# Five blocks of a macaron diffusion step become two: scans behind the input map, and one block from the heads' norm to the last norm

## The chip, the cores and the metric

The kernel runs on one core of a Trainium2 chip. The metric is device time in microseconds of that core for one execution. All data are float32; products that need more than the fast format gives are made of three matmuls of float32r halves (high and low parts).

## What is computed

One layer on 1152 tokens (128 context tokens, then 1024 latent tokens on a grid 64 wide), width 1024, 8 heads of 64, hidden width 2816:

```python
def trunk_layer(x, mod, s_fwd0, s_bwd0, grid, norm_w, ffn1_w13, ffn1_w2, ffn2_w13, ffn2_w2, mixer_params):
    m = mod[:, None].astype(x.dtype)
    h = rmsnorm(x, norm_w[0]) * (1.0 + m[:, :, 1]) + m[:, :, 0]
    x = x + 0.5 * m[:, :, 2] * swiglu(h, ffn1_w13, ffn1_w2)
    h = rmsnorm(x, norm_w[1]) * (1.0 + m[:, :, 4]) + m[:, :, 3]
    y, s_f, s_b = token_mixer(h, s_fwd0, s_bwd0, grid, *mixer_params)
    x = x + m[:, :, 5] * y
    h = rmsnorm(x, norm_w[2]) * (1.0 + m[:, :, 7]) + m[:, :, 6]
    x = x + 0.5 * m[:, :, 8] * swiglu(h, ffn2_w13, ffn2_w2)
    return x, s_f, s_b
...
    u = h @ w_in                       # in token_mixer
    o_f, s_f = wkv_scan(r_h, decay[:, :, 0], k_dir[:, :, 0], v_h, kk, a_h[:, :, 0], s_fwd0, False)
    o_b, s_b = wkv_scan(r_h, decay[:, :, 1], k_dir[:, :, 1], v_h, kk, a_h[:, :, 1], s_bwd0, True)
    o = o_f + o_b                      # then a norm per head, a bonus term and a gate g
    y_rwkv = o.astype(h.dtype) @ w_o_rwkv
    y_four = fourier_mix(f, grid) @ w_fourier
    merged = (gates[:, :, 0] * y_rwkv + gates[:, :, 1] * y_four).astype(h.dtype)
    return merged @ w_out, s_f, s_b
```

## The kernel before

Activations lie transposed: 128 channels on the partitions, the 1152 tokens along them, in three chunks of 384 tokens (`CH`) for the dense parts. `program` runs five stages. A stage is one block: each engine (PE, DVE, ACT, POOL and SP) has its own stream of instructions with hand-placed semaphore waits, and at the end of a block all engines meet at a barrier (`Kit.stage`); inside a block they meet only at semaphores.

1. `ffn` and `projection`, joined by `run`. The input map has 35 output rows, `p` = 0 to 34, each of three chunks with 24 matmuls (`product`, L1491). Rows 10 to 33 carry windows of six rows for each of four channel tiles `ct`, in which DVE makes the scans' four operands of a direction (`products`, L1358 to L1371) and SP stores them to the DRAM array `streams` (`store_operands`, L1109). The backward direction (d = 1) is made in window row 4, the forward one (d = 0) in window row 5, that is rows 32 and 33 for the last tile. PSUM banks 0 to 2 hold even rows, 3 to 5 odd ones.
2. `scans`: the RWKV recurrence by 128 tokens, 18 units (9 blocks of tokens in each direction, two chunks of 64 tokens in each), software-pipelined over slots `m` = -4 to 18. In slot m, unit m+4 gets its products within a chunk (`within`, PE L1915, and their masking `masked`, DVE L1803); POOL sends 16x16 blocks of them to DRAM and fetches them back as 64 lanes (`blocks_out` L1676, `lanes_in` L1684); unit m+3 has its triangular 16x16 blocks inverted by DVE (`row`, `corner`, L1826 to L1851); unit m+2 has them turned by ACT (`turn_block`) and taken through DRAM into `xy16` by SP (L1623, L1640), which also loads unit m+5 (`load_ar` L1604, `load_bkv` L1614); unit m+1 gets its inverse of 64x64 on PE, unit m its state update and output. POOL begins by clearing buffers (L1653 to L1659, semaphore `preset`), and PE, DVE and ACT wait for that; PE also waits for the initial states (`states_in`).
3. `head_norm`: norm per head, bonus and gate over 12 steps (`skewed`), beside it the feature half of the Fourier mixing (`channels`, 11 units on PE and ACT); SP loads its operands and the DFT matrices.
4. `fourier`: ACT and DVE split the matrices and `g` into halves (8 pairs, in `ORDER`), PE does a few two-column matmuls for the grid's edges (L2320, L2321), the context's 8 matmuls (L2325), then four groups q of 24 matmuls with 512 columns and two edge matmuls (L2337, L2342). ACT copies the odd part, DVE composes `whole`, ACT and DVE split it into `f_hi` and `f_lo` (L2403). SP reloads `x`.
5. `merge` (a `hidden_stage` on 8 tiles: products of both branches L936, times gates from DRAM, then `w_out` L951), the second `ffn` and `final_norm`, joined by `run`. It starts with SP's loads of raw weights (L755), their high halves (ACT L789) and low halves (DVE L825).

`run` writes the streams of several parts one after another on each engine, with no barrier between parts:

```python
def run(nc, parts):
    with nc.Block() as block:
        @block.sync
        def _(sp):
            for part in parts:
                part.sync(sp)
```

Of the kernel before, what the change touches and what calls it, by code (L numbers as in the profile page):

```python
# [691 lines left out]
def hidden_stage(kit, tag, tiles, ku, w_up, w_down, norm, moving, combine, gate, prev=None):  # L692
# [21 lines left out]
    with ExitStack() as ctx:  # L714
# [36 lines left out]
        def sync(sp):  # L751
# [29 lines left out]
        def scalar(act):  # L781
# [52 lines left out]
        def vector(dve):  # L834
# [36 lines left out]
            else:  # L871
                first_low(dve)

# [43 lines left out]
        def tensor(pe):  # L917
# [3 lines left out]
            def up(i, par, c, early):  # L921
# [9 lines left out]
                for j, q in enumerate("ab"):  # L931
                    hi, lo = moving[j]
                    for k in range(ku):
# [101 lines left out]
def projection(kit, mix, x_saved, cst, kd_sum, streams, v_back, g_last, prev):  # L1035
# [31 lines left out]
    with ExitStack() as ctx:  # L1067
# [22 lines left out]
        def sync(sp):  # L1090
# [24 lines left out]
            for p in range(J_END):  # L1115
# [8 lines left out]
                else:  # L1124
                    sp.wait_ge(evicted, p * 3 + 3)
# [40 lines left out]
                if w == 5:  # L1166
                    store_operands(ct, 0)
            for par in range(2):
                sp.wait_ge(row_stored[par], rows_before(par, J_END))
                sp.wait_ge(stored[par], 64 * CT)  # L1170
# [129 lines left out]
        def vector(dve):  # L1300
# [99 lines left out]
            for p in range(J_END):  # L1400
# [21 lines left out]
                if w == 5:  # L1422
# [99 lines left out]
    stage.engines(sync, scalar, vector, gpsimd, tensor)  # L1522
    prev.follow = norm
# [8 lines left out]
def scans(kit, cst, streams, v_rows, n_blocks, x_blocks, o, g_last, states_in, states_out):  # L1532
# [11 lines left out]
             "lane_step", "turned_block", "full6", "free6", "full7", "free7", "u_done", "u_act", "u_dve", "z_done",  # L1544
# [11 lines left out]
    with ExitStack() as ctx:  # L1556
        buf = lambda name, shape, dt=F32: ctx.enter_context(nc.sbuf_tensor("sc_" + name, shape, dt))
        masks = buf("masks", [P, MASK_W])
        ar = buf("ar", [P, AR, 2, CT, P])

        bk, vs = buf("bk", [P, BKV, CT, 4, CK]), buf("vs", [P, BKV, CT, P])
# [4 lines left out]
        q_plus, x_wide, y_wide, y = (buf(n, [P, HEADS, CK]) for n in ("q_plus", "x_wide", "y_wide", "y"))  # L1566
        a_tall = buf("a_tall", [P, CT, 2, HD])

        kb, uv = buf("kb", [P, 2, CT, 2, P]), buf("uv", [P, 2, CT, 2, 2, HD])
        wa = buf("wa", [P, 2, CT, CK])  # L1570
        lane_n, lane_x = buf("lane_n", [64, 2, BL * (BL + 1)]), buf("lane_x", [64, 2, 2, BL * (BL + 1)])
        prod, half_way = buf("prod", [64, 512]), buf("half_way", [64, 8, 8])
        z = buf("z", [P, 2, 2, CT, HD])
        zg = buf("zg", [P, 2, CT, HD])
        block = ctx.enter_context(nc.Block())
# [21 lines left out]
        @block.sync  # L1597
        def _(sp):
            sp.dma_start(masks[:], kit.dram["masks"]).then_inc(S["masks_in"], 16)

            def load_ar(k):
# [1051 lines left out]
```

## Time and profile before

| | |
|---|---|
| median of three runs | 3000.89 us (2998.18 to 3003.07) |
| profiled execution, its own time | 2998.46 us |
| its span, first to last instruction | 2996.6 us |
| PE busy | 2815.8 us (94%) |
| DVE, ACT, POOL busy | 1540.7, 805.5, 472.6 us |
| mean granted TensorE clock | 0.974 |
| block 1 to 2 (input map to scans) | last eviction starts 1445.04, first instruction of the next block 1450.35 |
| block 3 to 4 (heads' norm to Fourier) | last POOL operation starts 1852.11, next block 1854.20 |
| block 4 to 5 (Fourier to merge) | last DVE operation starts 1896.31, next block 1898.50 |

A busy engine is one with an instruction in flight, so gaps are what to look for. In a timeline row the columns are start (us), duration (us), engine, line, operation, output<-inputs, shapes and count; in brackets the idle time before it and what ended that. In the rows of DMA issues on SP and POOL the duration is that of issuing, and the landing comes later. The clock is given as a share of 2.4 GHz: 0.50 is 1.2 GHz.

### The profile page before, as it was taken

What the parts mean: (1) busy time and instruction counts of PE and PEld (TensorE: products, weight loads), DVE (VectorE), ACT (ScalarE), POOL (GpSimd) and SP (SyncE); (2) the same over time, 40 slices, a digit from 0 to 9 for tenths busy, and PEclk for the clock granted to TensorE, in tenths of its full rate; (3) what the DMA queues carried; (4) which work ended last, traced back from release to release, by engine and by line L of the source; (5) the groups of instructions that cost most, each with busy time, mean ns of one, the idle gap of its engine ahead of it and who ended that gap; (6) DMA issues with size and microseconds to landing.
All of it is one profiled execution on the core that took longest, in us unless ns stands there. A gap on an engine that the chain in (4) does not pass through costs nothing. (4 is left out here: it accounts for less than half of the span.)

```text
span 2996.6 us, 53527 instructions
## 1 busy us (share of the span) xinstructions
PE 2815.8 (94%) x21936; PEld 2684.9 (90%) x21936; DVE 1540.7 (51%) x2777; ACT 805.5 (27%) x1409; POOL 472.6 (16%) x569
## 2 busy tenths in 40 slices
PE   6999999999998998999599976899899999999998
PEld 3999999999997988999587865799799999999997
DVE  4456665566536345642377757445633333333335
ACT  4211111111115233444165544212511111111111
POOL 4101101110005010122234314122500000000001
PEclk9999999999999999999699998999999999999999
DMA  6122222222203434444545432321111111111112
GB/s 268 57 71 84 72 82 84 84 83 72 69 8 116 129 107 147 138 143 143 174 110 115 100 121 95 114 70 57 36 43 43 42 42 42 42 42 42 42 42 70
DMA packets 186302, 257.67 MB, mean 86 GB/s; under 512 B 98048, under 2 KB 136064, under 8 KB 184480
## 3 DMA queue, kind: packets, MB, share of 16 engines
q1 hardware_dynamic: 173280, 227.86, 23.3%
q0 software_dynamic: 12864, 27.54, 2.8%
q8 instruction: 119, 1.95, 0.3%
q14 instruction: 39, 0.32, 0.0%
HBM read 200.23 MB, written 55.12 MB: 85 GB/s over the span
## 5 line engine op out<-in xcount | busy, mean ns | idle before, releaser
L840 DVE SCALAR_TENSOR_TENSOR x<-bank,gate,x 128x128 f32<-128x128 f32 (+1 forms) x832 | 409.6, 515 | 200.0 <-PE bank L951 199.4
L1002 ACT ACTIVATE act_out_ffn<-bank 128x384 f32<-128x384 f32 x132 | 64.9, 491 | 1267.9 <-PE bank L936 1267.9
L1005 DVE TENSOR_TENSOR g_ffn<-act_out_ffn,bank 128x384 f32<-128x384 f32 x132 | 73.1, 554 | 616.6 <-ACT act_out_ffn L1002 616.6
L936 PE MATMUL bank<-h_hi_ffn,wlo_a_ffn 128*128 128x384 f32 x1056 | 359.2, 340 | 13.7 <-DVE h_lo_ffn L663 7.3
L936 PE MATMUL bank<-h_lo_ffn,whi_a_ffn 128*128 128x384 f32 x1056 | 356.8, 338 | 0.0
L936 PE MATMUL bank<-h_hi_ffn,whi_a_ffn 128*128 128x384 f32 x1056 | 356.7, 338 | 0.0
L936 PE MATMUL bank<-h_hi_ffn,whi_b_ffn 128*128 128x384 f32 x1056 | 355.2, 336 | 0.0
L936 PE MATMUL bank<-h_hi_ffn,wlo_b_ffn 128*128 128x384 f32 x1056 | 355.2, 336 | 0.0
L936 PE MATMUL bank<-h_lo_ffn,whi_b_ffn 128*128 128x384 f32 x1056 | 355.2, 336 | 0.0
L951 PE MATMUL bank<-g_hi_ffn,wlo_d_ffn 128*128 128x384 f32 x1056 | 354.4, 336 | 0.0
L951 PE MATMUL bank<-g_lo_ffn,whi_d_ffn 128*128 128x384 f32 x1056 | 353.1, 334 | 0.0
L951 PE MATMUL bank<-g_hi_ffn,whi_d_ffn 128*128 128x384 f32 x1056 | 353.1, 334 | 0.0
L1491 PE MATMUL bank<-h_hi_mix,wlo_in 128*128 128x384 f32 x840 | 292.9, 349 | 10.9 <-DVE wlo_in L1292 6.1
L1491 PE MATMUL bank<-h_lo_mix,whi_in 128*128 128x384 f32 x840 | 285.9, 340 | 0.0
L1491 PE MATMUL bank<-h_hi_mix,whi_in 128*128 128x384 f32 x840 | 285.5, 340 | 0.0
L936 PEld LDWEIGHTS bank<-h_hi_ffn,wlo_a_ffn 128*128 128x128 f32 x1056 | 199.9, 189 | 15.6 <-DVE h_lo_ffn L663 9.7
L936 PEld LDWEIGHTS bank<-h_lo_ffn,whi_a_ffn 128*128 128x128 f32 x1056 | 199.9, 189 | 0.1
L936 PEld LDWEIGHTS bank<-h_hi_ffn,whi_a_ffn 128*128 128x128 f32 x1056 | 199.7, 189 | 0.0
L951 PEld LDWEIGHTS bank<-g_lo_ffn,whi_d_ffn 128*128 128x128 f32 x1056 | 198.3, 188 | 0.5
L951 PEld LDWEIGHTS bank<-g_hi_ffn,wlo_d_ffn 128*128 128x128 f32 x1056 | 198.3, 188 | 0.5
L936 PEld LDWEIGHTS bank<-h_hi_ffn,whi_b_ffn 128*128 128x128 f32 x1056 | 198.6, 188 | 0.0
L936 PEld LDWEIGHTS bank<-h_lo_ffn,whi_b_ffn 128*128 128x128 f32 x1056 | 198.5, 188 | 0.0
(300 smaller groups left out, 4936.5 us busy)
## 6 DMA issues: line engine op xcount, KB each, us to landing
ada_beside_ffn<-in_ada_w POOLq DMA_DIRECT2D x96, 256.0 KB, 3.5
raw_a_ffn<-in_ffn_w SPq DMA_DIRECT2D x44, 512.0 KB, 4.5
raw_b_ffn<-in_ffn_w SPq DMA_DIRECT2D x44, 512.0 KB, 5.0
raw_d_ffn<-in_ffn_w SPq DMA_DIRECT2D x44, 512.0 KB, 3.6
raw_in<-in_w_in SPq DMA_DIRECT2D x35, 512.0 KB, 5.1
mix<-row_out SPq DMA_DIRECT2D x23, 576.0 KB, 3.2
sc_ar<-streams SPq DMA_DIRECT2D x36, 256.0 KB, 3.5
gates<-mix SPq DMA_DIRECT2D x16, 576.0 KB, 5.0
```

The lines of the kernel that those rows point to most:

```text
L840: ins = nc.vector.scalar_tensor_tensor(xs, kit.banks[4 + d % 4][:, a:b], kit.gate[:, gate, d, cond:cond + 1], xs, ALU.mult, ALU.add)
L936: mm = nc.tensor.matmul(kit.banks[2 * slot + j][:, 0:CH], w[q][:, par, cols], v[:, k, toks], start=(k == 0 and m == 0), stop=(k == ku - 1 ...
L951: mm = nc.tensor.matmul(kit.banks[4 + d % 4][:, 0:CH], w["d"][:, par, cols], v[par][:, c], start=(par == 0 and m == 0), stop=(par == 1 and ...
L1002: return self.nc.scalar.activation(out, a, ACT.Silu)
L1005: self.nc.vector.tensor_tensor(g32, act_out, b, ALU.mult).then_inc(g32_ready, 1)
L1491: mm = nc.tensor.matmul(bank[3 * par + c][:, 0:CH], wt[:, par, cols], v[:, k, toks], start=(k == 0 and m == 0), stop=(k == KT - 1 and m == 2))
```

## The change

The scans become a `Part` that follows the input map in the same block, and head norm, Fourier, merge, second FFN and last norm share one block. The barriers between go; waits on the semaphores of the part in front take their place.

- `projection`: the last tile's forward operands are made one row earlier (row 32 instead of 33). Before it waits for the last row, SP waits until all operands are stored and then loads unit 0, the masks and the initial states of the scans. The scans' buffers are laid out anew so that these lie clear of what the input map still uses. The last waits for stores move behind the scans (`rows_out`).
- `scans`: PE starts when the row before the last has been evicted; its waits for `preset` and `states_in` move to the first matmuls that need them. POOL's clearing starts when the last product is done. For units 0 and 1, ACT issues half of `blocks_out`. In slots -2 and -1, SP loads unit m+5 behind the `xy16` transfers, not ahead of them.
- `fourier`: PE does the context first, then the edges in the order q = 0, 3, 1, 2 with waits for the head norm's last users of those banks. ACT's splits wait for `gated` and `with_bonus`. SP's reload of `x` waits for `lo_ready`.
- `merge`: the first weights are loaded when the fourth Fourier group is done on PE.

```diff
@@ projection, sync
+                    if p == J_END - 1:
+
+                        for d in range(2):
+                            sp.wait_ge(stored[d], 64 * CT)
+                        stage.follow_loads(sp)
                     sp.wait_ge(evicted, p * 3 + 3)
...
-                if w == 5:
+                if w == (4 if ct == CT - 1 else 5):
                     store_operands(ct, 0)
@@ projection, vector
-                if w == 5:
+                if w == (4 if ct == CT - 1 else 5):
                     products(ct, 0)
@@ scans, sync
+        def first_loads(sp):
+            load_unit(sp, 0)
             sp.dma_start(masks[:], kit.dram["masks"]).then_inc(S["masks_in"], 16)
...
+        prev.follow_loads = first_loads
...
-                k = m + 5
...
+                if m >= 0 or m < -2:
+                    load_unit(sp, m + 5)
...
+                if -2 <= m < 0:
+
+                    load_unit(sp, m + 5)
@@ scans, gpsimd
+            for d in range(2):
+                pool.wait_ge(prev.stored[d], 64 * CT)
+            pool.wait_ge(prev.proj_done, J_END * NC)
...
-                for c in range(2):
+                for c in range(1 if k < 2 else 2):
@@ scans, scalar
+                if m + 4 < 2:
+                    act.wait_ge(S["am_ready"], 4 * (m + 4) + 4)
+                    for b in range(4):
+                        act.dma_start(*blocks_of(m + 4, 1, b)).then_inc(S["n_out_act"], 16)
@@ scans, tensor
-            pe.wait_ge(S["preset"], 7)
-            pe.wait_ge(S["states_in"], 32)
+
+            pe.wait_ge(prev.evicted, J_END * NC - 3)
@@ fourier, tensor
+            pe.wait_ge(prev.s["dft_in"], 32)
+            pe.wait_ge(prev.s["g_ready"], 11)
...
+            for q in (0, 3, 1, 2):
...
+                if q < 3:
+                    pe.wait_ge(prev.s[("rooted", "bonus_v", "gated")[q]], prev.steps)
@@ fourier, scalar
+            act.wait_ge(prev.s["with_bonus"], prev.steps)
+            act.wait_ge(prev.s["gated"], prev.steps)
@@ hidden_stage, sync, scalar and tensor
+            if after:
+
+                sp.wait_ge(after.s["done"], FG)
...
+                act.wait_ge(after.s["out_lo"], FG)
+                act.wait_ge(after.s["ctx_lo"], 1)
...
+                    if after and early and (par, c) == (0, 0):
+
+                        pe.wait_ge(after.before["lo_ready"], CT * NC)
+                        pe.wait_ge(*((after.s["out_lo"], FG) if j else (after.s["whole"], 5)))
@@ program
-                run(nc, [first, projection(kit, mix, x_saved, cst, kd_sum, streams, v_back, g_last, first)])
-            with kit.stage():
-                scans(kit, cst, streams, (mix[2 * CT:3 * CT], v_back), n_blocks, x_blocks, o, g_last,
-                      dram["states"], states_out)
+                second = projection(kit, mix, x_saved, cst, kd_sum, streams, v_back, g_last, first)
+                third = scans(kit, cst, streams, (mix[2 * CT:3 * CT], v_back), n_blocks, x_blocks, o, g_last,
+                              dram["states"], states_out, second)
+                run(nc, [first, second, third])
...
+            run(nc, [of_heads, mixed, merged, last, final_norm(kit, y_out, last)])
```

SP in slots -2 and -1 of the scans, before (`x_blocks` is unit 0's turned block on its way out, `sc_xy` its way back, `sc_ar`, `sc_bk`, `sc_vs` the load of unit 3, then the same of units 1 and 4):

```order
L1623 DMA x_blocks<-sc_lane_x 64x2x256
L1604 DMA sc_ar<-streams 128x4x128 x2
L1614 DMA sc_bk<-streams 128x4x64 x2
L1614 DMA sc_bk<-streams 128x4x128
L1614 DMA sc_vs<-v_back 128x4x64 x2
L1640 DMA sc_xy<-x_blocks 16x16x16 x8
```

and in the changed kernel:

```order
L1663 DMA x_blocks<-sc_lane_x 64x2x256
L1674 DMA sc_xy<-x_blocks 16x16x16 x8
L1630 DMA sc_ar<-streams 128x4x128 x2
L1640 DMA sc_bk<-streams 128x4x64 x2
L1640 DMA sc_bk<-streams 128x4x128
L1640 DMA sc_vs<-v_back 128x4x64 x2
```

The load of unit 3 has moved behind the eight transfers back of unit 0.

SP where the input map ends, in the changed kernel (the first row is the store of row 33, the last store of `mix` that of row 34; between them stands the load of unit 0, the masks and the states, which before stood behind the barrier):

```order
L1145 DMA mix<-row_out 128x1152
L1630 DMA sc_ar<-streams 128x4x128 x2
L1640 DMA sc_bk<-streams 128x4x64 x2
L1640 DMA sc_bk<-streams 128x4x128
L1640 DMA sc_vs<-mix 128x4x64 x2
L1653 DMA sc_masks<-in_masks 128x192
L1655 DMA sc_z<-in_states 128x256 x2
L1145 DMA mix<-row_out 128x1152
```

The load of the first unit has moved ahead of the last row's store.

PE at the end of the heads' norm, before (`hn_g_up` is the gate's matmul of the last step; the branches are the end of one block and the start of the next):

```order
L2155 MATMUL bank<-hn_gd,hn_g_up 128x384
L2096 UNCONDITIONAL_BRANCH
L2313 UNCONDITIONAL_BRANCH
L2320 MATMUL bank<-fo_dft,fo_g 128x2 x4
L2321 MATMUL bank<-fo_dft,fo_g_left 128x2
...
L2325 MATMUL bank<-fo_dft_ctx,fo_g_ctx 128x128 x8
```

and in the changed kernel:

```order
L2203 MATMUL bank<-hn_gd,hn_g_up 128x384
L2364 MATMUL bank<-fo_dft_ctx,fo_g_ctx 128x128 x8
L2374 MATMUL bank<-fo_dft,fo_g 128x2 x4
L2375 MATMUL bank<-fo_dft,fo_g_left 128x2
```

The eight context matmuls now come first, directly behind the last gate.

## Rows read from the trace of the kernel before

**Rows 1.** The page's 40 slices of 75 us: granted TensorE clock in tenths

```profile
PEclk9999999999999999999699998999999999999999
```

**Rows 2.** Stretches around joints: us, busy by engine (count), clock, DMA share, GB/s

```profile
1846.00:1850.00 4.00, 0.91 (x2) 0.30 (x2) 3.97 (x5) 1.23 (x2) 1.97 (x3) 0.62 0.00 0
1892.00:1903.00 11.00, 0.90 (x4) 0.29 (x2) 3.96 (x10) 2.91 (x4) 0.00 (x0) 0.63 0.26 85
1907.00:1909.00 2.00, 2.00 (x9) 2.00 (x9) 0.00 (x0) 0.00 (x0) 0.00 (x0) 0.65 1.04 426
```

**Rows 3.** Timeline of SP where the input map ends

```profile
1436.22 1.20 SPq L1109 DMA_DIRECT2D streams<-wo_keep  x1
```

**Rows 4.** Timeline of POOL where the scans begin

```profile
1450.35 0.56 POOL L1653 MEMSET sc_z<- 128x256 f32 x2 [50.23 <-POOLq L86]
...
1455.40 0.16 POOL L1659 MEMSET sc_lane_x<- 64x16 f32 x2
...
1465.91 4.24 POOL L1676 DMA_DIRECT2D n_blocks<-sc_nkr  x8 [6.62 <-DVE sc_nkr L1803]
```

**Rows 5.** Timeline of PE in the scans' first slots

```profile
1458.62 2.08 PE L1915 MATMUL bank<-sc_ar,sc_bk 64*128 64x128 f32 x16 [13.62 <-DMA sc_z<-in_states]
...
1489.88 2.08 PE L1915 MATMUL bank<-sc_ar,sc_bk 64*128 64x128 f32 x16 [4.67 <-DMA sc_vs<-v_back]
1492.63 0.37 PE L1928 MATMUL bank<-sc_xy,sc_n 64*64 64x64 f32 x2 [0.67 <-DMA sc_xy<-x_blocks]
```

**Rows 6.** Timeline of DVE from the input map's end on

```profile
1425.86 1.23 DVE L1292 TENSOR_TENSOR wlo_in<-raw_in,whi_in 128x1024 fp32r<-128x1024 f32 x1 [5.69 <-ACT whi_in L1177]
...
1460.85 1.29 DVE L1803 TENSOR_TENSOR sc_nkr<-bank,sc_masks 128x512 f32<-128x512 f32 x2 [28.50 <-PE bank L1915]
...
1473.72 0.16 DVE L1826 COPY sc_lane_x<-sc_lane_n 64x2 f32<-64x2 f32 x1 [1.69 <-DMA sc_lane_n<-n_blocks]
```

**Rows 7.** Timeline of SP in slot -2 of the scans

```profile
1481.61 0.62 SPq L1623 DMA_DIRECT2D x_blocks<-sc_lane_x  x1
...
1485.18 1.13 SPq L1614 DMA_DIRECT2D sc_vs<-v_back  x2
1486.35 4.57 SPq L1640 DMA_DIRECT2D sc_xy<-x_blocks  x8
```

**Rows 8.** DMA issues 1440 to 1512 us: queue, count, KB each, median us to landing

```profile
sc_vs<-v_back SPq DMA_DIRECT2D x4, 128.0 KB, 3.9
...
x_blocks<-sc_lane_x SPq DMA_DIRECT2D x3, 128.0 KB, 2.4
```

**Rows 9.** ACT's copy once per slot: min/median/max ns, first and last start

```profile
L1699 ACT ACTIVATE sc_a_tall<-bank x18: 597/597/605, 1499.6 to 1760.3; 128x512 f32<-128x512 f32 x18
```

**Rows 10.** Timeline of PE, heads' norm to merge

```profile
1846.07 0.91 PE L2155 MATMUL bank<-hn_gd,hn_g_up 128*128 128x384 f32 x2 [2.30 <-DVE x L2242]
1854.25 1.84 PE L2320 MATMUL bank<-fo_dft,fo_g 128*128 128x2 f32 x8 [7.26 <-PEq L86]
...
1863.47 3.79 PE L2325 MATMUL bank<-fo_dft_ctx,fo_g_ctx 128*128 128x128 f32 x16
1866.91 0.72 PE L2337 MATMUL bank<-fo_dft_hi,fo_g_lo 128*128 128x512 f32 x1
...
1892.51 0.39 PE L2342 MATMUL bank<-fo_left_rows,fo_left_hi 2*128 2x512 f32 x1
1903.36 0.66 PE L936 MATMUL bank<-rwkv_hi,wlo_a_merge 128*128 128x384 f32 x1 [10.46 <-DVE wlo_b_merge L825]
```

**Rows 11.** Timeline of ACT where the Fourier stage begins

```profile
1854.22 0.63 ACT L2348 ACTIVATE fo_dft_hi<-fo_dft 128x512 fp32r<-128x512 f32 x1 [2.20 <-PEq L86]
```

**Rows 12.** Timeline of DVE, last bonus, last Fourier half, first weights of the merge

```profile
1850.91 0.56 DVE L2242 TENSOR_TENSOR x<-bank,hn_v 128x384 f32<-128x384 f32 x1 [0.92 <-POOL hn_v L2259]
...
1896.31 1.23 DVE L2403 TENSOR_TENSOR fourier_lo<-fo_whole,fourier_hi 128x1024 fp32r<-128x1024 f32 x1 [1.12 <-ACT fourier_hi L2348]
...
1902.52 0.69 DVE L825 TENSOR_TENSOR wlo_b_merge<-raw_b_merge,whi_b_merge 128x512 fp32r<-128x512 f32 x1
```

More of the change, by code:

```diff
@@ L689, in vector, with hidden_stage @@
                 normed(m + DEEP)
-def hidden_stage(kit, tag, tiles, ku, w_up, w_down, norm, moving, combine, gate, prev=None):
+def hidden_stage(kit, tag, tiles, ku, w_up, w_down, norm, moving, combine, gate, prev=None, after=None):
     nc = kit.nc
@@ new lines, in blocks_of, with load_ar, load_bkv @@
+        def blocks_of(k, c, b):
+            at = 64 * c + BL * b
+            return (n_blocks[k, :, c, b].rearrange("h s t -> s h t"),
+                    nkr[at:at + BL, k % NKR, :, :, c, 0, BL * b:BL * b + BL].rearrange("s e x t -> s (e x) t"))
+        def load_ar(sp, k):
+            for q in range(2):
+                sp.dma_start(*ar_of(k, q)).then_inc(ar_loaded[k % AR], 16)
+        def load_bkv(sp, k):
+            at = slice(k // 2 * P, k // 2 * P + P)
+            b, key, v = (src[:, :, at].rearrange("c p t -> p c t")
+                         for src in (streams[k % 2, 2], streams[k % 2, 3], v_rows[k % 2]))
+            pieces = [(bk[:, k % BKV, :, 3 * c], b[:, :, CK * c:CK * (c + 1)]) for c in range(2)]
+            both = bk[:, k % BKV].rearrange("p c q t -> p c (q t)")[:, :, CK:3 * CK]
+            for dst, src in pieces + [(both, key)] + [(vs[:, k % BKV, :, half(1 - c)], v[:, :, half(c)]) for c in range(2)]:
+                sp.dma_start(dst, src).then_inc(bkv_loaded[k % BKV], 16)
@@ L2084, in _ @@
                     ins.then_inc(S["wy_done"], 1)
+    part = Part()
+    part.engines(sync, scalar, vector, gpsimd, tensor)
+    return part
 def head_norm(kit, cst, mix, o, kd_sum, o_hi, o_lo, waves):
@@ L2243, in _, with gpsimd @@
             skewed([(0, center), (2, bonus), (3, gated), (1, normed)])
-            dve.wait_ge(s["lo_ready"], steps)
-        @block.gpsimd
-        def _(pool):
+        def gpsimd(pool):
             for ct in range(CT):
@@ L2265, in _ @@
             skewed([(0, weighted), (2, with_bonus), (3, low)])
+    part_of = Part()
+    part_of.engines(sync, scalar, vector, gpsimd, tensor)
+    part_of.s, part_of.steps = s, steps
+    return part_of
 class Waves:
@@ L2322, in _ @@
                                  skip_group_check=True)
-            for q in range(FG):
-                for p in range(2):
-                    ins = nc.tensor.matmul(bank[3][:, q * P:(q + 1) * P], waves.g_ctx[:, p, q], waves.dft_ctx[:, p],
-                                           start=(p == 0), stop=(p == 1))
-            ins.then_inc(s["ctx_done"], 1)
             for q in range(FG):
@@ L2404, in _, with gpsimd @@
                     .then_inc(s["out_lo"], 1)
-            dve.wait_ge(s["out_lo"], FG)
-            dve.wait_ge(s["ctx_lo"], 1)
+        def gpsimd(pool):
+            pass
+    part = Part()
+    part.engines(sync, scalar, vector, gpsimd, tensor)
+    part.s, part.before = s, prev.s
+    return part
 class Merge:
```

152 lines of the change are left out of this document (70 added, 82 removed).

## Prediction

> **What bounds the kernel now.** The page's clock row comes first: 40 slices, 9 in all but three, and one 6, at 1423 to 1498 us, where the input map gives way to the scans [rows 1]. With PE 94% busy, the dense stages offer nothing to this change. It can win only where PE stands still, at the joints, so I read the timelines of all engines there, each from the last work of one stage to the first full work of the next.
>
> At the first joint POOL begins to clear buffers at 1450.35, though the input map's last eviction began at 1445.04, and is done at 1455.56 [rows 4]. PE does its first product of a unit at 1458.62, held by the initial states, which SP asks for behind the barrier [rows 5]. DVE masks it at 1460.85 [rows 6], POOL spends 4.24 us on eight issues of blocks [rows 4], and the inversion starts at 1473.72 [rows 6]. From there one engine hands to the next until the slots run. ACT's copy, once per slot, goes from 1499.6 to 1760.3 in 17 steps, 15.3 us each [rows 9]: the recurrence is a chain, and the change keeps its order from slot 0 on.
>
> At the heads' norm's end PE's last gate starts at 1846.07; then it idles 7.26 us, does edges for 9.22 us (1854.25 to 1863.47), the context in 3.44 (to 1866.91), and meets its first dense matmul at 1866.91 [rows 10]. ACT waits for the same barrier [rows 11]. From Fourier to merge, DVE's last half starts at 1896.31 and runs 1.23; PE gets its first weights at 1903.36 after 10.46 us idle, DVE's low half being last [rows 10, 12]. The barrier between heads' norm and scans stays.
>
> **The change, joint by joint.** Sums are against the profiled execution, 2998.46 us.
>
> *Input map to scans.* POOL's clearing takes 5.21 us (1450.35 to 1455.56) [rows 4]. Started at 1445.1, when the last product is done, it ends at 1450.3. SP's stores of operands end about 1438 (the last issue begins at 1436.22 and takes 1.20) [rows 3]. The loads of unit 0, now issued behind them, take 4.1 us to issue (1486.35 - 1481.61 - 0.62 for unit 3) and 3.9 to land [rows 7, 8]; with masks and states they are in by about 1447, and PE's first products (2.08 us) are done under the clearing. So the first mask can start at 1450.3 in place of 1460.85: 10.5 us gained. POOL and ACT now share unit 0's eight issues: half of 4.24 is 2.1; I give back 0.3, since ACT's half needs the last mask as POOL's does. The inversion then starts 12.3 us sooner, near 1461.4.
>
> Against that: in slot -2 SP issued unit 0's block at 1481.61, unit 3's loads, the last two (1.13 together) at 1485.18, and the transfers back (4.57) at 1486.35 [rows 7]; PE took unit 3 at 1489.88, held 4.67 by those loads [rows 5], 8.3 us after the first issue. Now the loads stand behind the transfers back, which wait for the block to land: 2.4 [rows 8], eight issues 4.57, the loads up to the last one 1485.18 - 1481.61 - 0.62 = 2.95, and 0.57, its landing 3.9 [rows 8]: 14.4 us. Unit 3 comes 6.1 us later against unit 0. It holds what stands behind it on PE, unit 0's inverse among them; the 0.67 that PE waited for the transfer back [rows 5] goes. Joint: -12.3 + 6.1 - 0.7 = **-6.9 us**. Unit 4 is needed a slot of 15.3 later, and covered. Bounds: nothing given back and the transfer gained is -13; the loads as late again is -1.
>
> The transfers out and back have no load beside them now. The rows' 2.4 us is taken with such loads. The Trainium skill (DMA: Bandwidth & Descriptors, Latency and other measured facts) puts the access to HBM at 0.2 us on average and 2 us at high load. By the page, an estimate, the block would land up to 1.8 sooner, and the joint give -8.7. No row of before shows that transfer alone.
>
> Making the last tile's forward operands in row 32 costs nothing: DVE idles 5.69 us before 1425.86 [rows 6], and the products are off PE's path. Were that cover gone, four products of 1152 columns, 1.4 each by the 1.23 that 1024 take [rows 6], would delay PE 5.5 at most. The row stores at the scans' end lie behind the barrier's own work, on SP alone. ACT's four new issues per unit, 2.1 us, fall in slots in which it idles.
>
> *Heads' norm to Fourier.* PE can go on after 1846.98 with the context, 3.44 us, to 1850.4, then 9.22 of edges to 1859.6; the last of its new semaphores comes when DVE's gating ends, 1850.91 + 0.56 [rows 12], ahead of need. ACT's splits wait for the same and begin about 1852.0 in place of 1854.22 [rows 11], and stay ahead of PE. That is 7.3 sooner than 1866.91. But the clock is 0.62 on average in 1846 to 1850 [rows 2], and PE's ten microseconds of two-column matmuls follow it. Before, the 128-column context stood directly ahead of the dense part; now the edges do. So the first dense matmuls run at 1.2 GHz for longer. The merge shows the price: its dense work begins at 1903.36 [rows 10], and the clock still averages 0.65 over 1907 to 1909, PE being full [rows 2], so about 5 us are done at half speed, against some 0.5 here before. 4.5 us at half speed lose 2.2. **-5.1 us**; bounds -8.4 (clock up, ACT's start sets it) and -4.5.
>
> *Fourier to merge.* The last low half ends at 1897.54 [rows 12]. The raw weights, asked for when PE's fourth group is done, 1892.51 + 0.39 [rows 10], land by 1896.8 at the latest, by the 2.4 to 3.9 of rows taken elsewhere [rows 8]; ACT's high halves are done about as DVE's last Fourier half is, and DVE's two low halves behind its last Fourier half, 0.69 each or less [rows 12], let PE start at 1899.0 (1897.54 + 0.69 + 0.69, and 0.1). That is **-4.4 us**. PE is busy 0.90 of 11 us at a clock of 0.63 before [rows 2], and would still start low. Bounds -4 and -6.5 (clock up: half of 5 us less).
>
> Sum: -6.9 - 5.1 - 4.4 = **-16.4 us**, 2982.1 in the profiled execution's terms. That execution is 2.4 under the median of 3000.89; the four executions shown average 3000.2. Minus 16.4 that is 2983.7, and I say **2983.5 us**.
>
> **The rivals.**
>
> *More of the scans' start is gained.* If the loads queued behind the transfers are not what PE next needs, because DVE's inversion of unit 1 or the slot itself is last, the joint gives -13: total -22.5, 2977.5 us. For it: 4.67 us of PE's wait [rows 5] fell in a stretch where PE has little. Against: `within` of unit 3 stands ahead of unit 0's inverse on PE.
>
> *The clock comes back.* With idle gaps of 6 in place of 10.46 us [rows 10], it may hold: -6.9 - 8.4 - 6.5 = -21.8, 2978 us. Against: 0.62 right after the gate [rows 2].
>
> *The scans keep less.* If two loads hold PE, unit 4's too, joint one gives -3: -12.5, 2987.5 us.
>
> *The change does not do what it says.* The early loads wait for stores; every microsecond by which they land after 1450.3 is one lost. Were they as late as the states were (PE at 1458.62, 8 us), the joint gives about +1: total -8.5, 2991.5 us. Against: the stores' last issue at 1436.22 leaves 14 us.
>
> *Slower: SP becomes the bound of the slots.* The scans now hold the row stores' semaphores, a new layout of buffers and a loop changed on SP. Were each of the 17 steps [rows 9] longer, 0.96 us would cancel the whole, and from 1.3 us (16.4 + 6 = 22.4) it is slower by over 0.2%; at 1.6 us a step it gives +10.8, 3011 us. Against: SP's slot of 1481.61 to 1490.92 is 9.3 us of work [rows 7] in 15.3, and the order from slot 0 on is unchanged.
>
> **How the numbers follow.** A measurement of this kernel tells about 0.2%, 6 us, from no change. Forecast 0.60, with 2979 to 2988 as its own range; more gained 0.14; clock back 0.10; less kept 0.07; not as said 0.03; slots longer 0.06, half of it under 1.3 us a step, counted as no change. All but the last are faster by over 6 us: faster 0.94, same 0.03, slower 0.03. The range 2973 to 2989.5 reaches to both gains together and to the smaller one.
>
> **What would show it.** DVE's first mask near 1450.3 behind POOL's clearing; the first inversion near 1461.4; PE's unit 3 waiting for its loads, 14 us behind the first block's issue; ACT's copies still 15.3 apart, 6.9 us earlier. PE's first dense Fourier matmul 13 us after the last gate, in place of 20.8, at a clock of 0.5, and the merge's first matmul 1.5 us after DVE's last Fourier half. The forecast is wrong if the copies' distance changes, if unit 3 waits for nothing, or if the clock is near 1 at either of the later joints.

## The result and the profile after

| | before | changed |
|---|---|---|
| median | 3000.89 us | 2982.28 us (five runs, 2978.81 to 2985.01) |
| ratio, 95% interval | | 0.9934 (0.9916 to 0.9951) |
| span of the profiled execution | 2996.6 us | 2978.6 us |
| PE busy, its share | 2815.8 us (94%) | 2812.2 us (94%) |

The change gave 18.6 us of the medians and 18.0 us of the spans. PE's busy time fell by 3.6, so most of the gain came out of PE's idle time, at the joints. The table adds the two spans up, from mark to mark. Every mark is the start or end of a row. The *inversion* is DVE's work on the triangular blocks (its copy into `sc_lane_x`), the *last gate* is the head norm's last pair of `hn_g_up` matmuls, and a *Fourier group* is one of the four rounds of dense 512-column matmuls.

| stretch | before | changed | difference |
|---|---|---|---|
| start to the input map's last matmul | 1445.00 | 1443.28 | -1.7 |
| from there to DVE's first mask | 15.85 | 5.46 | -10.4 |
| to the first inversion | 12.87 | 12.37 | -0.5 |
| to PE's first `sc_xy` matmul (unit 0's inverse) | 18.91 | 23.92 | +5.0 |
| to ACT's first copy per slot | 6.92 | 5.20 | -1.7 |
| to ACT's second copy | 14.55 | 17.41 | +2.9 |
| to its last | 246.22 | 247.13 | +0.9 |
| to the last gate of the heads' norm | 85.75 | 85.96 | +0.2 |
| to the end of the first Fourier group | 27.58 | 19.42 | -8.2 |
| to the end of the fourth | 19.25 | 19.21 | 0.0 |
| to the merge's first matmul | 10.46 | 5.95 | -4.5 |
| to the end | 1093.24 | 1093.29 | 0.0 |

The first row is not the change's: the difference is the same 1.75 us in ACT's rows from 1145 us on, long before anything that the diff touches. Over the kernels below, whose input map is the same, the mark lies anywhere from 1443.2 to 1445.7.

POOL at the scans' start (start, duration, instruction, and in brackets the idle time before it with its releaser):

```profile
1443.43 0.56 POOL L1693 MEMSET sc_z<- 128x256 f32 x2 [45.03 <-PE bank L1509]
...
1448.48 0.16 POOL L1699 MEMSET sc_lane_x<- 64x16 f32 x2
...
1453.79 2.17 POOL L1714 DMA_DIRECT2D n_blocks<-sc_nkr  x4 [4.58 <-DVE sc_nkr L1843]
1459.03 0.55 POOL L1722 DMA_DIRECT2D sc_lane_n<-n_blocks  x1 [3.07 <-DMA n_blocks<-sc_nkr]
```

The clearing starts 0.15 us behind the last matmul, where it stood 5.35 behind [rows 4], and DVE's first mask follows it at once:

```profile
1424.14 1.23 DVE L1310 TENSOR_TENSOR wlo_in<-raw_in,whi_in 128x1024 fp32r<-128x1024 f32 x1 [0.41 <-ACT whi_in L1195]
1448.74 1.29 DVE L1843 TENSOR_TENSOR sc_nkr<-bank,sc_masks 128x512 f32<-128x512 f32 x2 [23.37 <-POOL sc_lane_x L1699]
...
1461.11 0.16 DVE L1866 COPY sc_lane_x<-sc_lane_n 64x2 f32<-64x2 f32 x1 [1.19 <-DMA sc_lane_n<-n_blocks]
```

Ahead of 1424.14 DVE idled 0.41 us, where it idled 5.69 [rows 6]: the operands now made in row 32 fill that gap, as predicted, and the input map's end is not later for it.

PE's first product is done far ahead of that, since SP has fetched its operands while the input map still ran. SP, from the last store of the scans' operands on:

```profile
1429.00 1.18 SPq L1121 DMA_DIRECT2D streams<-wo_keep  x1
...
1434.94 0.99 SPq L1630 DMA_DIRECT2D sc_ar<-streams  x2
...
1440.00 0.91 SPq L1655 DMA_DIRECT2D sc_z<-in_states  x2
...
1468.94 0.62 SPq L1663 DMA_DIRECT2D x_blocks<-sc_lane_x  x1
1471.36 3.79 SPq L1674 DMA_DIRECT2D sc_xy<-x_blocks  x8
1475.19 1.01 SPq L1630 DMA_DIRECT2D sc_ar<-streams  x2
...
1477.96 1.45 SPq L1640 DMA_DIRECT2D sc_vs<-v_back  x2
```

The last store is issued at 1429.00, 7.2 us sooner than before [rows 3]. The load of unit 0 is issued from 1434.94 to 1439.3, the states to 1440.9. Later, unit 0's turned block goes out at 1468.94, comes back from 1471.36 on, and only then are the loads of unit 3 issued. PE shows what that costs:

```profile
1443.21 1.16 PE L1954 MATMUL bank<-sc_ar,sc_bk 64*128 64x128 f32 x16
...
1483.02 2.08 PE L1954 MATMUL bank<-sc_ar,sc_bk 64*128 64x128 f32 x16 [10.40 <-DMA sc_vs<-v_back]
```

It waited 10.40 us for unit 3, 14.1 behind the block's issue (1468.94 to 1483.02), in place of 4.67 and 8.3 [rows 5, 7]. ACT's copy, once per slot (min, median and max in ns, first and last start):

```profile
L1736 ACT ACTIVATE sc_a_tall<-bank x18: 597/597/598, 1490.2 to 1754.8; 128x512 f32<-128x512 f32 x18
```

By the table the 17 steps sum to 264.5 us, against 260.8, and 2.9 of the 3.8 lie in the first of them.

PE from the last gate to the end of the first Fourier group:

```profile
1840.73 0.91 PE L2203 MATMUL bank<-hn_gd,hn_g_up 128*128 128x384 f32 x2 [2.31 <-DVE x L2287]
1841.48 3.29 PE L2364 MATMUL bank<-fo_dft_ctx,fo_g_ctx 128*128 128x128 f32 x16
1844.56 1.28 PE L2374 MATMUL bank<-fo_dft,fo_g 128*128 128x2 f32 x8
...
1846.08 1.05 PE L2374 MATMUL bank<-fo_dft,fo_g 128*128 128x2 f32 x8
...
1847.37 1.05 PE L2374 MATMUL bank<-fo_dft,fo_g 128*128 128x2 f32 x8
...
1848.66 1.87 PE L2374 MATMUL bank<-fo_dft,fo_g 128*128 128x2 f32 x8
...
1850.97 0.80 PE L2386 MATMUL bank<-fo_dft_hi,fo_g_lo 128*128 128x512 f32 x1
...
1858.53 0.50 PE L2386 MATMUL bank<-fo_dft_hi,fo_g_lo 128*128 128x512 f32 x1 [0.24 <-DVE fo_g_lo L2429]
...
1859.76 0.39 PE L2391 MATMUL bank<-fo_left_rows,fo_left_hi 2*128 2x512 f32 x1
```

The context's matmuls come right behind the gate. Three of the four edge groups take 1.28 to 1.05 us, the fourth 1.87, as all four did before [rows 10]. The clock shows why (columns as in [rows 2]):

```profile
1841.00:1845.00 4.00, 4.00 (x21) 3.73 (x21) 3.62 (x4) 1.25 (x3) 1.97 (x3) 0.60 0.01 4
1845.00:1849.00 4.00, 4.00 (x30) 3.90 (x30) 1.79 (x4) 3.04 (x7) 2.50 (x3) 0.93 0.16 13
1851.00:1855.00 4.00, 4.00 (x11) 3.17 (x11) 3.70 (x7) 4.00 (x9) 0.00 (x0) 0.50 1.02 415
1885.00:1889.00 4.00, 3.69 (x12) 3.72 (x13) 0.21 (x1) 0.00 (x0) 0.00 (x0) 0.50 1.02 411
```

The 0.60 during the context is a mean: the clock was still at 1.00 for the last gate, fell to 0.50 within the context, and was back at 1.00 in the first edge group. It is 0.93 in the first three, and 0.50 again when the dense matmuls begin. Between the fourth group and the merge:

```profile
1878.97 0.39 PE L2391 MATMUL bank<-fo_left_rows,fo_left_hi 2*128 2x512 f32 x1
1885.31 0.66 PE L948 MATMUL bank<-rwkv_hi,wlo_a_merge 128*128 128x384 f32 x1 [5.95 <-DVE wlo_a_merge L830]
```

PE idles 5.95 us in place of 10.46 [rows 10]; the merge still begins at 0.50.

### The profile page after: what moved, and what is told of

It is laid out like the page before. It is cut to its first block and busy times, and to the rows that moved or that the text cites. A ratio compares the mean times of both kernels' runs of the same rounds, so it can differ in the third digit from the quotient of the medians.

```text
span 2978.6 us, 53460 instructions
## 1 busy us (share of the span) xinstructions
PE 2812.2 (94%) x21936; PEld 2680.6 (90%) x21936; DVE 1541.9 (52%) x2777; ACT 805.3 (27%) x1409; POOL 468.7 (16%) x561
## 3 DMA queue, kind: packets, MB, share of 16 engines
q8 instruction: 119, 1.95, 0.3%
## 5 line engine op out<-in xcount | busy, mean ns | idle before, releaser
L948 PE MATMUL bank<-h_hi_ffn,wlo_a_ffn 128*128 128x384 f32 x1056 | 358.8, 340 | 11.3 <-DVE h_lo_ffn L663 4.5
L948 PEld LDWEIGHTS bank<-h_hi_ffn,wlo_a_ffn 128*128 128x128 f32 x1056 | 199.6, 189 | 13.2 <-DVE h_lo_ffn L663 6.8
```

The source lines that it names most:

```text
L948: mm = nc.tensor.matmul(kit.banks[2 * slot + j][:, 0:CH], w[q][:, par, cols], v[:, k, toks], start=(k == 0 and m == 0), stop=(k == ku - 1 ...
```

## The experiments

Executions of one kernel lie 1 to 10 us apart, so medians of four or five runs do not tell 3 us apart. The kernel before was run again beside each set (medians 3000.63, 2998.53 and 2999.36 us), so where two changed kernels are compared, their ratios are the fairer numbers. Most verdicts below are read from stretches between marks in the profiles, one profile for each kernel. Three are used: *front*, from the input map's last matmul to ACT's second copy per slot (69.10 before, 64.36 changed); *gate to group*, from the last gate to the end of the first Fourier group (27.58 and 19.42); *gap*, from the fourth group's end to the merge's first matmul (10.46 and 5.95).

**1. Units 3 and 4 loaded ahead of the transfers back.**

```diff
-                if m >= 0 or m < -2:
-                    load_unit(sp, m + 5)
+                load_unit(sp, m + 5)
...
-                if -2 <= m < 0:
-                    load_unit(sp, m + 5)
```

> The changed kernel with one part undone: in slots -2 and -1 SP again issues the loads of units 3 and 4 ahead of the transfers back. Theory A (PE's wait for unit 3's load is what the new order costs, 14.1 us behind the first block's issue against 8.3 before): unit 3's first product comes again about 8.3 us behind that issue, 5.8 sooner than in the changed kernel, but the transfer back then lands about 4 us later than it does there, so unit 0's inverse starts near 1480 in place of 1485.0 and the second of ACT's copies per slot is 3 to 5 us sooner. Time 2978 to 2980 us. Theory B (DVE's inversions and POOL's blocks set the first slots whatever SP does): that copy moves by less than 1 us, time 2982 us, or later by the transfers' delay.

Median 2974.40 us, ratio to the kernel before 0.9915 (0.9892 to 0.9937). PE's unit 3:

```profile
1477.46 2.08 PE L1950 MATMUL bank<-sc_ar,sc_bk 64*128 64x128 f32 x16 [4.74 <-DMA sc_vs<-v_back]
```

That is 8.4 us behind the block's issue at 1469.05. Unit 0's inverse starts 11.3 us behind it in place of 16.1, front 57.25. Against 64.36 that is 7.1 less; against the mean of the four kernels with the front unchanged (64.36 and the 62.13, 60.33 and 60.99 of experiments 5 to 7: 61.95) 4.7. Experiment 12 has the same edit, and there the front was 59.06, 2.9 below that mean. Theory A holds, and this part of the change costs more than it brings: 3 to 5 us.

**2. The same loads still earlier**, behind that of unit 2 (`if m == -3: load_unit(sp, 3); load_unit(sp, 4)`).

> The changed kernel with the loads of units 3 and 4 issued in slot -3, right behind that of unit 2 and ahead of the first block's turn, into buffers that are free then. Theory A: PE waits for neither load; unit 0's inverse waits only for its transfer back, 8 to 9 us behind the first block's issue, near 1477.5 in place of 1485.0; the second of ACT's copies comes 5 to 8 us sooner, time 2975 to 2977 us. Theory B: less than 1 us of it arrives. If the early loads delay the small block transfers, the first inversion itself (12.5 us behind the first mask) comes later.

Median 2977.21 us, ratio 0.9925 (0.9905 to 0.9945). PE waited for neither load, and the inverse started 8.2 us behind the block's issue, as theory A has it. But the first inversion came 15.5 us behind the first mask, not 12.4: POOL's store of the blocks met the loads.

```profile
1455.92 2.16 POOL L1714 DMA_DIRECT2D n_blocks<-sc_nkr  x4 [4.57 <-DVE sc_nkr L1843]
1462.39 0.54 POOL L1722 DMA_DIRECT2D sc_lane_n<-n_blocks  x1 [4.31 <-DMA n_blocks<-sc_nkr]
```

POOL waits 4.31 us for them to land, where 3.07 stood. Front 60.06, 4.3 us less than changed and not the 5 to 8 expected: part of the gain went back into the small transfers.

**3. POOL alone issues the block stores** (ACT's four issues and their semaphore taken out, POOL's loop over both chunks).

> The changed kernel with POOL issuing all eight block stores of units 0 and 1, ACT none. As predicted the shared issue is worth 1.8 us from first mask to first inversion. The trace of the changed kernel shows that stretch as 12.37 us (1448.74 to 1461.11) against 12.87 before (1460.85 to 1473.72), 0.5 us. So by the prediction the stretch goes to 14.2 us, by the trace to 12.9. Time within 2 us of the changed kernel either way.

Median 2979.42 us, ratio 0.9934 (0.9916 to 0.9953). The stretch from first mask to first inversion is 12.98 us. Sharing the issues is worth 0.6 us, not the 1.8 predicted: POOL issues for 4.23 us and then waits 1.50 for the landing here, 2.17 and 3.07 in the changed kernel. The issues took half the time, and most of the rest went into the wait.

Experiment 11 shows what the wait was for. It shares the issues too, but holds unit 2's load until these blocks have landed:

```profile
1455.74 2.17 POOL L1714 DMA_DIRECT2D n_blocks<-sc_nkr  x4 [3.52 <-DVE sc_nkr L1845]
...
1459.40 0.55 POOL L1722 DMA_DIRECT2D sc_lane_n<-n_blocks  x1 [1.50 <-DMA n_blocks<-sc_nkr]
```

POOL waits 1.50 us, and the stretch is 11.09 us, 1.9 less than with POOL alone. In the changed kernel SP issues unit 2's load from 1449.67 to 1455.0, just ahead of and beside the shared stores (1453.79 to 1455.96); POOL's last stores in experiment 3 go out some 2 us later. So the predicted 1.8 us is there when no load is in flight, and unit 2's load takes most of it away.

**4. The masks do not wait for the clearing.**

```diff
@@ scans, vector
-            dve.wait_ge(S["preset"], 7)
+            for d in range(2):
+                dve.wait_ge(prev.stored[d], 64 * CT)
+            dve.wait_ge(prev.proj_done, J_END * NC)
...
                 if s == 6:
+                    if k == 0:
+                        dve.wait_ge(S["preset"], 7)
```

> The changed kernel with DVE's masks no longer waiting for POOL's clearing, only for the input map's last product and stores; the first inversion waits for the clearing instead. If the clearing is what the scans' start waits for, the first mask comes about 5 us sooner (right behind PE's first product, near 1444 in place of 1448.7), the first inversion 4 to 5 us sooner, and the time is 4 to 5 us less, 2978 us. Rival: PE's first products or the loads of units 1 and 2 are late next, or PE's hold for unit 3 (its loads stand behind the block's transfer) passes it on in full; if unit 1's load is late the gain is 1 to 2 us.

Median 2978.18 us, ratio 0.9929 (0.9909 to 0.9949). The first mask starts 1.23 us behind the last matmul, the first inversion 16.47 behind it (DVE, then PE):

```profile
1445.55 1.29 DVE L1845 TENSOR_TENSOR sc_nkr<-bank,sc_masks 128x512 f32<-128x512 f32 x2 [19.16 <-PE bank L1958]
...
1460.79 0.15 DVE L1870 COPY sc_lane_x<-sc_lane_n 64x2 f32<-64x2 f32 x1
```

```profile
1444.24 1.16 PE L1958 MATMUL bank<-sc_ar,sc_bk 64*128 64x128 f32 x16
...
1454.60 2.08 PE L1958 MATMUL bank<-sc_ar,sc_bk 64*128 64x128 f32 x16 [6.54 <-DMA sc_vs<-v_back]
```

Of 4.2 us gained at the mask, 1.4 arrive at the inversion: PE waits 6.54 us for unit 1's load, and unit 0's blocks land among the loads (POOL waits 4.31 us, as in experiment 2). The rival named beforehand, a gain of 1 to 2 us, is what happened.

**5. Edges ahead of the context**, as before the change.

> The changed kernel with the edges' two-column matmuls again ahead of the context's in the Fourier stage, nothing else changed. Theory A (the splits set the end of the first Fourier group: its last operand half was ready only when PE reached it, 0.24 us waited for DVE at 1858.53, so a slow clock on PE costs nothing there): the stretch from the last gate to the end of the first group stays 19.0 us within 1 us. Theory B (PE with its clock sets it): edges at 1.2 GHz cost 3 us more than the mix seen, dense matmuls at 2.4 GHz give 2.4 back or less, and the order moves the end by more than 1 us.

Median 2978.05 us, ratio 0.9926 (0.9909 to 0.9944). Gate to group 20.28 us: 0.9 more. All four edge groups ran at 1.2 GHz, and the dense matmuls sooner at 2.4. That is within the 1 us of theory A, but DVE was not waited for at all in the first group, so PE set the end here. The clock, 2 us behind the last gate and 14 us behind it (columns as in [rows 2]):

```profile
1844.66:1846.66 2.00, 2.00 (x10) 1.97 (x10) 1.89 (x4) 0.75 (x2) 0.18 (x1) 0.50 0.00 0
1856.66:1858.66 2.00, 2.00 (x9) 1.55 (x9) 2.00 (x5) 1.81 (x4) 0.00 (x0) 0.87 1.03 424
```

The other kernels with the changed order show both. PE in experiment 1:

```profile
1834.58 3.13 PE L2360 MATMUL bank<-fo_dft_ctx,fo_g_ctx 128*128 128x128 f32 x16
1837.50 1.71 PE L2370 MATMUL bank<-fo_dft,fo_g 128*128 128x2 f32 x8
...
1839.65 1.87 PE L2370 MATMUL bank<-fo_dft,fo_g 128*128 128x2 f32 x8
```

Here the clock fell and did not come up again in the context (1.71 and 1.87 for the first two edge groups), nothing waited for a split, and gate to group was 21.78; so it was in experiment 12. In experiment 2 the clock did not fall in the context at all:

```profile
1837.04:1839.04 2.00, 2.00 (x14) 1.73 (x15) 2.00 (x1) 0.50 (x1) 1.79 (x2) 1.00 0.00 0
```

PE waited for DVE's halves there, and gate to group was 19.42. The nine other kernels that keep order and joint, the changed one and experiment 2 among them, lie at 19.40 to 20.34: seven at 19.40 to 19.42, all with a wait for DVE's halves in the first group, and two (experiments 4 and 9) at 20.3 with none. So the splits set a floor of 19.4, and the clock adds 0 to 2.4 us. The order by itself is not shown to cost anything, since its 20.28 lies inside that spread. Why the clock was back by the first edge group in nine executions and not in two was not settled.

**6. Extra matmuls in the gap**: 26 of 512 columns into bank 4, read from the heads' halves; they compute nothing that is used.

```diff
@@ fourier, tensor, at its end
+            pe.wait_ge(prev.s["lo_ready"], prev.steps)
+            pe.wait_ge(s["whole"], 5)
+            for _ in range(26):
+                nc.tensor.matmul(bank[4][:], kit.spare[:, 0, 0:P], kit.spare[:, 0, 0:512], start=True, stop=True)
```

> The changed kernel with 26 extra 512-column matmuls at the end of PE's Fourier part, about 5.6 us of work without use, into a bank that nobody reads, in the 5.95 us in which PE idles ahead of the merge. If the idle PE is what makes the clock fall, it stays at 2.4 GHz and the merge's first 4 us of work at 1.2 GHz take 2: 2 to 2.4 us less up to the second row of the merge, time 2980 us. If the clock falls all the same, or the extra work ends later than the weights come, 0 or up to 1 us more.

Median 2975.64 us, ratio 0.9926 (0.9909 to 0.9942). The gap and the merge's start, 7 and 4 us:

```profile
1876.00:1883.00 7.00, 7.00 (x31) 5.26 (x30) 4.06 (x10) 2.70 (x4) 0.00 (x0) 1.00 0.72 249
1883.00:1887.00 4.00, 4.00 (x25) 4.00 (x25) 0.00 (x0) 0.00 (x0) 0.00 (x0) 1.00 1.03 420
```

The clock is 1.00 where it was 0.50, and from the merge's first matmul to its second row of output it took 13.17 us in place of 15.17, the 2.0 us expected, with the gap unchanged at 5.96. The kernels without extra work, before and after the change, lie at 14.6 to 15.9 in that stretch (mean 15.4), those with it (experiments 10 to 12 too) at 13.2 to 14.4 (mean 13.7). In experiment 10 PE then waited 1.63 us for the second row's weights, so a part of the gain met a wait.

**7. The two rear barriers back.**

```diff
@@ program
-            run(nc, [of_heads, mixed, merged, last, final_norm(kit, y_out, last)])
+            tail = final_norm(kit, y_out, last)
+            run(nc, [of_heads])
+            run(nc, [mixed])
+            run(nc, [merged, last, tail])
```

> The changed kernel with the two barriers back between heads' norm, Fourier and merge, the order on each engine unchanged. The two stretches from last gate to the end of the first Fourier group (19.0 us, 27.2 before) and from last Fourier group to first merge matmul (6.3, 10.9 before) should give back most of 8.2 and 4.5 us if the barrier is the cause: 10 to 13 us more, time 2992 to 2995 us. If the order on PE (context ahead of edges, which brings the clock up) gave a part of the 8.2, that part stays: then 7 to 9 us more.

Median 2988.76 us, ratio 0.9968 (0.9957 to 0.9979). Gate to group 25.63, gap 9.79: 6.2 and 3.8 us given back, 10.0 in all. The ratios give 10 us too (0.9968 against 0.9934), the low end of the 10 to 13 expected; the median rose by 6.5, less than expected. The remaining 1.95 us of the first and 0.7 of the second are not the barriers': the order on PE and the waits, and what a stage's end did beyond the barrier, were not tried for them.

What a barrier costs here is mostly what it holds back. At the first, POOL's last operation ran to 1841.94, and only then could PE begin the context and ACT the splits (1842.70):

```profile
1840.95 0.99 POOL L2306 TENSOR_TENSOR rwkv_lo<-x,rwkv_hi 128x384 fp32r<-128x384 f32 x1 [0.27 <-ACT rwkv_hi L2249]
1842.74 3.36 PE L2364 MATMUL bank<-fo_dft_ctx,fo_g_ctx 128*128 128x128 f32 x16 [6.52 <-PEq L108]
```

At the second, SP could ask for the merge's weights only at 1884.70, when DVE's last half was done (1884.43); without the barrier it asked at 1879.39, as soon as the fourth group had ended.

**8. A barrier back between input map and scans**, early loads kept (the last hunk of experiment 9's diff).

> The changed kernel with a barrier back between input map and scans; unit 0's loads, masks and states stay early. By the prediction the loads' share is what held PE before, and the barrier's own share is small: clearing starts when the last eviction is over, about 5 us later than now (before: 1450.35 against an eviction from 1445.04, in place of 0.1 us after the last product), so the scans' start gives back 5 to 6 us and no more, time 2987 to 2988 us. Rival: without the barrier's gain nothing of the 12.6 us is left, time 2994 us.

**9. The same, and unit 0's loads, masks and states behind the barrier.**

```diff
@@ projection, sync
-                        stage.follow_loads(sp)
@@ scans, sync
         def sync(sp):
+            first_loads(sp)
@@ program
-                run(nc, [first, second, third])
+                run(nc, [first, second])
+                run(nc, [third])
```

> The changed kernel with a barrier between input map and scans and, behind it, unit 0's loads, masks and states (the run before this one with a barrier alone had them early: 6.8 us from the input map's last matmul to the first mask, in place of 5.5). By the kernel before (first product 8.3 us behind the barrier, mask 10.5) the loads are the larger share: from last matmul to first mask 11.5 to 12 us, so early loads are worth 5 us and the barrier 1.3. The rest of the 15.9 us of the kernel before (4 us) would be what its block end waits for: the stores' landing and the clearing of semaphores. Rival: the 15.9 comes back in full, then the barrier's cost depends on what hangs on it.

Medians 2979.40 us, ratio 0.9938 (0.9921 to 0.9955), and 2988.30 us, 0.9961 (0.9948 to 0.9973). DVE's first mask with the barrier alone, then PE's first product and DVE's first mask with the loads late too:

```profile
1450.27 1.29 DVE L1843 TENSOR_TENSOR sc_nkr<-bank,sc_masks 128x512 f32<-128x512 f32 x2 [24.70 <-POOL sc_lane_x L1699]
```

```profile
1454.75 2.08 PE L1954 MATMUL bank<-sc_ar,sc_bk 64*128 64x128 f32 x16 [9.64 <-DMA sc_vs<-mix]
```

```profile
1456.97 1.29 DVE L1843 TENSOR_TENSOR sc_nkr<-bank,sc_masks 128x512 f32<-128x512 f32 x2 [29.78 <-PE bank L1954]
```

From last matmul to first mask: 5.46 us changed, 6.77 with the barrier, 11.86 with late loads, 15.85 in the kernel before. So of the 10.4 us gained, the barrier between blocks is 1.3, the early loads 5.1, and the last 4.0 is what the old stage's end did besides. The trace places it ahead of the scans' first instruction, which starts 1.54 us behind the last matmul (1445.11) in experiment 9 and 5.35 behind it in the kernel before [rows 4]:

```profile
1446.65 0.56 POOL L1693 MEMSET sc_z<- 128x256 f32 x2 [46.42 <-POOLq L108]
```

What it consists of is read from the program: waiting for the last stores, clearing the stage's semaphores, and a second barrier behind that (`all_engine_barrier` in `Kit.stage`). These were not tried apart. My expectation for the barrier, 5 to 6 us, was wrong: I had taken the old stage's end for the price of a barrier.

**10 to 12. Towards a faster version.** The tenth holds unit 2's load on SP until the first lanes have landed (`sp.wait_ge(n_in[0], 16)` in slot -3), together with experiments 1, 4 and 6; the eleventh adds unit 1's load to the early ones; the twelfth is experiments 1 and 6 alone.

> Four edits on the changed kernel: masks wait no longer for the clearing; SP holds unit 2's load until the first lanes have landed (so that the small block transfers meet fewer loads: they took 4.3 us to land with three loads issued on end, 1.5 before); units 3 and 4 are loaded ahead of the transfers back; 26 extra matmuls ahead of the merge. From last matmul to first inversion 17.8 us now, 16.5 with early masks alone: expected 13 to 14.5. From last matmul to ACT's second copy 60 to 64 now; expected 53 to 55. With 2 us at the merge, 10 us less in all: 2971 us. If unit 1's load, behind the last row's store, still holds PE (6.5 us with early masks), the first inversion comes no sooner than 16 us.

> As the four edits, and unit 1's load too ahead of the last row's store. PE's hold for unit 1 (6.5 us with early masks) should go, and the landing of unit 0's blocks meet no large load: first inversion 12 to 13 us behind the last matmul, ACT's second copy 51 to 53, time 2969 us. Rival: the last row's store and the small transfers are late next, and nothing is gained over holding unit 2 alone.

> The two edits that gained by themselves, put together: units 3 and 4 loaded ahead of the transfers back (4.3 us less up to ACT's second copy than the median of the kernels with the changed order) and 26 extra matmuls ahead of the merge (2.0 us less in its first row). They lie in different stages, so they should add: 6 us less than the changed kernel, 2974 to 2976 us; ratio to the kernel before 0.991 to 0.992.

| | median, ratio to before | first inversion behind last matmul | front | gate to group | merge's first row |
|---|---|---|---|---|---|
| changed | 2982.28, 0.9934 | 17.83 | 64.36 | 19.42 | 15.17 |
| 10 | 2972.89, 0.9914 (0.9899 to 0.9930) | 16.10 | 55.65 | 19.40 | 14.35 |
| 11 | 2973.03, 0.9916 (0.9902 to 0.9929) | 16.23 | 57.62 | 19.41 | 13.53 |
| 12 | 2974.01, 0.9915 (0.9901 to 0.9928) | 17.86 | 59.06 | 21.78 | 13.79 |

All three beat both kernels in their medians, the tenth by 9.4 us against the changed one (6.0 by the ratios), though the intervals of the two ratios overlap. The times expected were 2971, 2969 and 2974 to 2976 us, so the tenth and eleventh came 2 and 4 us later. The edits did not add up as I expected. In the tenth, unit 1's load still holds PE 6.16 us, and the inversion comes at 16.1, not 13 to 14.5. In the eleventh it is the masks that land late, since they stand behind unit 1's load on SP: the first mask starts 5.14 us behind the last matmul in place of 1.24. Its small transfers do land fast, with no load beside them (experiment 3). The twelfth has the front of experiment 1 and its clock that stays down after the last gate, so its 2974 us is no proof that the two edits add.

## Why the prediction was right, point by point

The forecast was 2983.5 us for 2982.28, -16.4 for the -18.0 of the spans. That the sum fits so well is partly luck: two terms were off, one each way, and 1.7 of the 18.0 were gained ahead of the change, in the table's first row.

- **Scans' start.** The first mask was put 10.5 us sooner and came 10.4 sooner, for the reasons given: clearing at once, loads under the input map. The shared issue was put at 1.8 and is 0.5 to 0.6 (experiment 3). The step that failed is "half of 4.24", which counts the issuing alone: the landing ends that wait, and in the changed kernel unit 2's load is in flight beside it. With that load held back the gain was 1.9 (experiment 11). The price of unit 3's loads was put at +6.1, its product 14.4 us behind the block's issue; it came 14.1 behind it, and experiments 1 and 2 show cause and size. The joint was to give -6.9 and gave -7.6 to ACT's first copy and -4.7 to the second. The 2.9 us between is one step of 17.4 us in the one profile; in it PE idles three times with no releaser (2.8 us together). The seven other kernels with these loads behind the transfers took 14.5 to 15.9 for that step, so most of it belongs to the execution. Over the four kernels with this front the mean is -7.1.
- **The block's landing.** It took 2.4 us with no load beside it:

```profile
x_blocks<-sc_lane_x SPq DMA_DIRECT2D x1, 128.0 KB, 2.4
```

  That is what it took with loads queued behind it [rows 8]. The Trainium skill (DMA: Bandwidth & Descriptors, Latency and other measured facts) puts the access to HBM at 0.2 us on average and 2 us at high load, and the prediction's estimate from it was up to 1.8 us less; this row does not agree. The block stores do agree with it: 3.6 us among large loads (experiment 2), 1.8 with none in flight (experiment 11).

```profile
n_blocks<-sc_nkr POOLq DMA_DIRECT2D x4, 8.0 KB, 3.6
```

```profile
n_blocks<-sc_nkr POOLq DMA_DIRECT2D x4, 8.0 KB, 1.8
```

- **Heads' norm to Fourier.** Put at -5.1, bounds -4.5 and -8.4; it gave -8.2. The wrong step is "ten microseconds of two-column matmuls follow" a clock that has fallen, 9.22 us of edges: the clock was back at 1.00 in the first edge group, and the edges took 6.4 (1844.56 to 1850.97). It was so in nine of the eleven kernels with the context first (in three of them it had not fallen in the context at all), while with the edges first it stayed at 0.50 through all of them (experiment 5). The price of 1.2 GHz for the dense part, put at 2.2, was there (the first group took 9.2 us, before 6.7), but part of it lay over DVE's splits, which set the floor (experiment 5). ACT began them 5.9 us behind the last gate (1846.60), as put. In the two kernels in which the clock stayed down, the joint gave -5.8, near the forecast. The rival "the clock comes back" was half right: it came back under the edges, not for the dense part. That is a part of the prediction's last sign of being wrong, a clock near 1 at a later joint.
- **Fourier to merge.** Put at -4.4, it gave -4.5. Experiment 7 gives 3.8 of it to the barrier, and experiment 6 shows the clock's price as 2.0 us, where I had half of 5 us.
- **Slots.** The distance of ACT's copies stayed: 247.1 us for the last 16 steps, against 246.2. Over the twelve kernels of the experiments it was 244.8 to 249.3 in eleven and 252.6 in experiment 9, whose profiled execution was its slowest (2992.08 us). The table's 0.9 is well inside that spread, and no run shows the rival in which SP bounds the slots.
- **Early loads late.** That rival falls too: PE's first product started at 1443.21, 5.5 us before anyone needed it. The last store was issued at 1429.00, since row 33's were moved to row 32; the prediction had counted with the old 1436.22. With stores 7.2 us later that product would have come up to 1.7 us too late, an estimate from these rows (1443.21 + 7.2 against 1448.74).

## What to carry to other kernels

Where stages meet, cost three things apart: the barrier itself (1.3 us between input map and scans), what the stage's end waits for and clears (4.0), and loads that could have been issued before it (5.1); the last two are the larger. The same barrier costs more where one engine is still at work and the others, or the next loads, must wait for it: 6.2 and 3.8 us at the two later joints. Small transfers that something waits for are best sent when no large load is in flight (1.9 us here in place of 0.6). When a load is moved to clear the way for a small transfer, ask who consumes the load next: here the transfer came back sooner and the engine stood still for the load, 5.8 us longer. And at an engine's idle gap of some 6 us, the price is the gap and the low clock behind it: about 2 us here, recovered by idle work.

## What was not expected of the hardware

- 26 useless matmuls in an idle gap of 5.95 us keep the granted clock at 1.00, where the dense work behind the gap otherwise begins at 0.50 (experiment 6, on again in 10 to 12).
- The same instructions behind the same 2.3 us of idle time met three clocks in eleven kernels: at 1.00 through the whole context (experiments 2, 8 and 10), fallen to 0.50 in it and back by the first edge group (six), and at 0.50 up to the dense part (experiments 1 and 12). Up to 2.4 us lie between them.
- Block stores of 8 KB land in 1.8 us alone and in 3.6 among loads of 128 and 256 KB. A second queue on ACT halves the issue time (4.23 to 2.17 us); it gave 0.6 us with unit 2's load in flight and 1.9 with none.
- A barrier between two blocks with the same semaphores costs 1.3 us where only the last eviction and its store are left; the end of a stage, with stores to wait for and semaphores to clear, 5.3.
